# A transformer forward pass on one core: another order of smaller steps in the recurrence, matrix-memory and sliding-attention stages, and the causal mask added by TensorE

## The chip, the core and the metric

The kernel is one program on 1 core of a Trainium2 chip. Time is device time of that core in microseconds (us). The time before is 3654.07 us, the median of 3 runs (3653.0 to 3654.23). Each engine runs its own list of instructions: TensorE (PE in the profile) multiplies matrices into PSUM, VectorE (DVE) and ScalarE (ACT) do the rest of the arithmetic, and SyncE (SP) issues the DMAs. They wait for each other through semaphores only.

## The reference, cut to what matters

256 positions of width 1024, all in float32. Two layers of a first block, each a `token_mixing` and a feed-forward part, then four layers of a second block. All weights are used once.

```python
# first block, layers l = 0, 1: token_mixing (branches a, b, c, d), then a feed-forward part
proj = (rmsnorm(x, g_pre) * (1 + scale) + shift) @ w_in
p = causal_softmax(q1 k1^T / 8) - lam * causal_softmax(q2 k2^T / 8)   # a: 4 differential heads
ya = (rmsnorm(p v, g_subln) * (1 - lam_init)) @ da_w_o
q = [q_nope, rope(q_rope)]; k = [k_nope, rope(k_rope)]                # b: 8 latent heads, 64 + 32 wide
yb = (causal_softmax(q k^T / sqrt(96)) v_b) @ mla_w_o
yc = (sc_b * dwconv(sc_c * sc_u, 3 taps)) @ sc_w_o
yd = silu(layernorm(dwconv(cf_a * sigmoid(cf_g), 31 taps))) @ cf_w_o
x += gate1 * rmsnorm((g0*ya + g1*yb + g2*yc + g3*yd) @ w_mix_out)
# second block, layers n = 0..3
h = x + 0.5 * swiglu(rmsnorm(x));  h = h + mixer_n(rmsnorm(h));  h = h + 0.5 * swiglu(rmsnorm(h))
x = h + sigmoid(rmsnorm(h) @ w_ple_gate) * (p @ w_ple_proj)
# mixer 0 and 3, gated recurrence, 8 heads of 128, chunks of 64:
#   b = cumsum(log_f);  A[t,s] = sum_k q[t,k] k[s,k] exp(b[t,k] - b[s,k]) for s <= t
#   o = (q exp(b)) S + A v;  S = exp(b_last) S + (k exp(b_last - b))^T v
#   out = (rmsnorm(o) * silu(og)) @ w_out
# mixer 1, matrix memory, 4 heads: exponential input and forget gates, normalised by a running maximum
# mixer 2, sliding attention: 16 query heads, 4 key heads, window 128, distance bias, a sink per head
```

## The kernel before, in words

**Weights.** Every product is float32 by three passes. A weight tile of 128x1024 lands by a DMA of SyncE in one of 11 slots (`land`, NL, L278). ScalarE copies it into `whi`, one of 6 slots (NH; `split_scalar`, L401); VectorE subtracts that copy from the tile into `wlo` (`split_vector`, L413); TensorE multiplies high by high, high by low and low by high parts (`mm3`, L449 to L451). A "pair" is two such tiles: one projection of 128 rows of outputs over 256 positions, twice, 48 matmuls (`proj_tensor`, L466). To "take" a tile, ScalarE and VectorE split up to five tiles ahead (LOOK, L417; `take_scalar`, `take_vector`, L428), and the sixth slot is free only when TensorE has finished the tile that was in it.

**Steps.** The stages run one after the other: first block m0, f0, m1, f1 (mixing and feed-forward), then for n = 0 to 3 a half feed-forward (ha), the mixer (mx), the other half (hb) and the gate (pl). Within a mixer, all engines walk one list of steps: MIX (`mix_steps`, L891) for m0 and m1, HGRN (`hgrn_steps`, L1853) for mx0 and mx3, MLSTM (`mlstm_steps`, L2293) for mx1 and SWA (`swa_steps`, L2569) for mx2. Each engine issues its own instructions of a step in the order of the list and waits for events of others (`done` and `when`), so the list alone sets the order on TensorE, VectorE and ScalarE, and that of the weight tiles (`weight_order`, L3042). A PSUM bank's next writer waits for the event that its last user names (`Banks.use`, L177).

**Gated recurrence (HGRN).** Heads are worked in two groups of four. Per group: two pairs each for q (step q), the forget gate (f) and the values (v); `prepare` (wide elementwise work on decays); products across chunks, which use the state (`cross64`, `cross128`); seven `level` steps that build A by halves (ScalarE exponentials, VectorE differences and products, L2104 to L2119, small matmuls at L1942, and VectorE's mask and sum, L2254); `diagonal`; `values` (L1955). Then per head pair an output gate (gate, one pair), sums for the heads' norms (sum, L1965), `factor`, and `finish`, of which VectorE's low part is L1370. The norm ahead of the stage ends on TensorE at L1695. The order before, a dot standing for group and number:

```
norm q0.0 q0.1 f0.0 f0.1 v0.0 v0.1 prepare0 q1.0 cross64:0 q1.1 cross128:0 level0.0 f1.0 level0.1 f1.1 level0.2 v1.0
level0.3 v1.1 level0.4 0.5 0.6 diagonal0 values0 prepare1 sum0 sum1 factor0 cross64:1 gate0 cross128:1 level1.0 1.1 1.2
gate1 level1.3 finish0 level1.4 finish1 level1.5 gate2 level1.6 diagonal1 values1 sum2 sum3 factor1 gate3 finish2
finish3 end
```

**Matrix memory (MLSTM).** Projections qk (four pairs) and v (four), gate rows and columns, then per head `weights`, `scores`, `values`, `gate` and `tail` (norm and output gate of the head, L2528 to the low part at L1372), pipelined: gate i stands behind scores i+1, tail i behind values i. Order before: norm qk0 rows qk1 qk2 qk3 columns weights0 v0 v1 v2 v3 scores0 weights1 values0 scores1 weights2 values1 scores2 weights3 gate0 tail0 values2 scores3 gate1 tail1 values3 gate2 tail2 gate3 tail3 end.

**Sliding attention (SWA).** Three projections, per-head norm factors (`factor`) and transposes (`turn_in`, L2636) of them, then for each of 16 heads `scores` (L2646), `exp`, `turn` and `values`, and `heads` and `turn_out` at the middle and the end. Order before: norm proj0 columns proj1 factor0 turn_in0 factor1 turn_in1 proj2, then the heads, the four steps of a head one place apart.

**First-half mixers (MIX).** For each of four differential heads TensorE writes the scores of two blocks of 128 queries into 384 columns of a bank (L1065, L1066), VectorE adds a 384-column mask on the way out of PSUM (`softmax_vector`, L1357) and takes maxima from that copy (L1360, L1361), and ScalarE exponentiates it in place (`exp_scalar`, L1181). The bank is free after the mask addition ("masked"). Rope multiplies by a rotation in the bank MISC, which the norms' sums share (`rope_vector`, L1408, L1419); ScalarE's copies of the keys (L1321) follow the last rope.

Of the kernel before, what the change touches and what calls it, by code (L numbers as in the profile page):

```python
# [15 lines left out]
T = 256  # L16
# [28 lines left out]
def _plan_consts():  # L45
    at = 0
    for name, n in [("ident", 128), ("ones", 128), ("ones64", 128), ("mask3", 384), ("dist3", 384),
                    ("maskT", 128), ("lev", 192), ("rot", 96), ("inv", 1), ("rst", 256), ("spare", 15)]:
# [6 lines left out]
def constants():  # L55
# [10 lines left out]
    put("mask3", np.concatenate([causal, np.zeros((128, 128)), causal], 1))  # L66
# [195 lines left out]
class Program:  # L262


    def __init__(self, nc, ctx, args, order):
# [29 lines left out]
        self.sc = sb("sc", 16)  # L295
        self.ps = [ctx.enter_context(nc.psum_tensor(f"ps{i}", [128, 512], F32)) for i in range(8)]
# [262 lines left out]
def start_scalar(g, act):  # L559
# [3 lines left out]
    act.activation(g.small[:, 570:578], g.par[:, c:c + 8], ACT.Exp, scale=-1.0).then_inc(*D_("c_exp"))  # L563
    row_scalar(g, act)
# [326 lines left out]
def mix_steps():  # L891
# [27 lines left out]
    def merge(branch):  # L919
        return [[(f"wo{branch}", i), (f"gate{branch}", i)] for i in range(4)]  # L920
# [9 lines left out]
    for j in range(2):  # L930
        add("v", j)
        conv(2)
    add("tables")
    work = [[("mla", 0)], [("mla", 1)], [("mc", 0)]]
    work += alternate([[("mla_square", 0)], [("mla_norm", 0)], [("mla_square", 1)], [("mla_norm", 1)]],
                      [[("scu", j)] for j in range(4)] + [[("scb", j)] for j in range(2)])
    for n in range(2):
        work += [[("gate2", 2 * n)], [("gate2", 2 * n + 1)], [("wo2", 2 * n)], [("wo2", 2 * n + 1)]]
# [9 lines left out]
    add("ya_norm", 0)  # L948
    for r in range(4):
# [4 lines left out]
    add("ya_norm", 1)  # L954
    add("rope", 3)
# [8 lines left out]
    work = alternate([[("gate1", j)] for j in range(4)], [[("cf_mean", 0)], [("cf_norm", 0)]]) + merge(0) + merge(3)  # L964
    heads(8, ["mla_scores", "mla_scale", "mla_turn", "mla_values"], lambda: some(work, 1))
    some(work, len(work))
    for i in range(4):
        add("wo1", i)
    for j in range(4):
        add("out", j)  # L970
# [36 lines left out]
def mix_tensor(g, pe, st, lay):  # L1007
# [3 lines left out]
    for step, i, bank in MIX:  # L1011
# [42 lines left out]
        elif step in ("da_scores", "mla_scores"):  # L1054
# [4 lines left out]
            for m in range(2 if kind == "a" else 1):  # L1059
                b = 3 + m if kind == "a" else 3 + i % 2  # L1060
                pe.wait_ge(*W(*g.banks.use(b, "masked", st, kind, i, m)))
# [2072 lines left out]
```

## Time and profile before

| | |
|---|---|
| median of 3 runs | 3654.07 us |
| profiled execution, its own time | 3641.96 us |
| its span | 3639.9 us |
| mean granted TensorE clock | 0.948 |
| TensorE busy | 3291.6 us, 90% |
| VectorE busy | 2496.5 us, 69% |
| ScalarE busy | 1758.8 us, 48% |

| Stage | us in the span | TensorE idle, us |
|---|---|---|
| m0, m1 | 36.7 to 450.1, 659.1 to 1057.5 | 59.5, 52.1 |
| mx0, mx3 (gated recurrence) | 1446.0 to 1654.4, 3190.6 to 3405.2 | 50.7, 55.2 |
| mx1 (matrix memory) | 2071.9 to 2227.7 | 26.0 |
| mx2 (sliding attention) | 2645.9 to 2772.4 | 17.2 |

How to read it: the span is one profiled execution, from first to last instruction. Busy is the time in which an engine works on an instruction. The granted clock is a share of full speed, 2.4 GHz; 0.5 is 1.2 GHz. "x <- y" behind a time is what an engine waited for before it.

### The profile page before, as it was taken

Reading aid. Unit: us, or ns where it says so; the run is one execution under the profiler, and the core shown is the slowest. Engines: PE = TensorE matmul, PEld = TensorE weight load, DVE = VectorE, ACT = ScalarE, POOL = GpSimd, SP = SyncE. Lnnn points to the kernel's source line nnn. Section 1 sums busy time; section 2 is a strip of 40 time slices with the busy share of each in tenths; the row PEclk is TensorE's granted clock in tenths of the full one; section 3 lists DMA queues with packets and bytes.
Section 4 is the critical chain, followed back from the end, with each engine's and each line's share of the span. In section 5 each row is a group of like instructions: output and inputs, shape, how many; then the busy total and the mean of one; then the engine's idle time right before and its main releaser. Section 6 shows DMA issues by size and latency. Waiting matters only on the chain.

```text
span 3639.9 us, 64372 instructions
## 1 busy us (share of the span) xinstructions
PE 3291.6 (90%) x27058; PEld 3178.2 (87%) x27058; DVE 2496.5 (69%) x3768; ACT 1758.8 (48%) x2641; POOL 3.0 (0%) x6
## 2 busy tenths in 40 slices
PE   6788899887989999869999997999989999985898
PEld 6778899876989999759999987999968999985898
DVE  8877689886666766756676566666666666686656
ACT  4445444454544445555454445454455454464544
POOL 0000000000000000000000000000000000000000
PEclk9889999998999999979999999999989999997999
DMA  8444488443546565415656534655623655641453
GB/s 303 123 136 166 163 297 300 143 128 111 169 145 209 174 187 182 136 47 182 186 164 185 167 116 136 186 180 171 187 95 127 185 178 174 186 145 53 148 186 116
DMA packets 163920, 598.06 MB, mean 164 GB/s; under 512 B 18192, under 2 KB 18224, under 8 KB 163376
## 3 DMA queue, kind: packets, MB, share of 16 engines
q1 hardware_dynamic: 163632, 593.94, 51.1%
q8 instruction: 215, 3.52, 0.4%
q14 instruction: 73, 0.60, 0.1%
HBM read 592.82 MB, written 1.05 MB: 163 GB/s over the span
## 4 chain that ended last, share of the span: by engine, by line
PE 70%; DVE 21%; ACT 6%; issue 2%; DMA 1%; SPq 0%; DVEq 0%; ACTq 0%
PE ps L449 22%; PE ps L450 22%; PE ps L451 22%; DVE wlo L413 6%; DVE fa L1462 2%; ACT whi L401 2%; DVE hl L1666 1%; PE ps L622 1%; DVE land L506 1%; DVE tmps L530 0%; ACT L522 0%; DVE tmps L528 0%; DVE tmps L1804 0%; PE ps L712 0%; DMA land<-w_ada 0%
## 5 line engine op out<-in xcount | busy, mean ns | idle before, releaser
L449 PE MATMUL ps<-hh,whi 128*128 128x256 f32 (+1 forms) x5472 | 1561.4, 285 | 80.7 <-DVE hl L1666 32.8
L450 PE MATMUL ps<-hl,whi 128*128 128x256 f32 (+1 forms) x5472 | 1550.1, 283 | 0.0
L451 PE MATMUL ps<-hh,wlo 128*128 128x256 f32 (+1 forms) x5472 | 1545.1, 282 | 0.0
L413 DVE TENSOR_TENSOR wlo<-land,whi 128x1024 fp32r<-128x1024 f32 (+1 forms) x1032 | 1218.8, 1216 | 271.1 <-ACT whi L401 270.2
L449 PEld LDWEIGHTS ps<-hh,whi 128*128 128x128 f32 (+1 forms) x5472 | 1048.9, 192 | 93.3 <-issue 65.2
L401 ACT ACTIVATE whi<-land 128x1024 fp32r<-128x1024 f32 (+1 forms) x1032 | 1028.9, 1044 | 174.6 <-PE ps L451 161.5
L450 PEld LDWEIGHTS ps<-hl,whi 128*128 128x128 f32 (+1 forms) x5472 | 1048.9, 192 | 0.9
L451 PEld LDWEIGHTS ps<-hh,wlo 128*128 128x128 f32 (+1 forms) x5472 | 1048.0, 192 | 0.0
L449 PE MATMUL ps<-ra,whi 128*128 128x256 f32 (+1 forms) x2416 | 691.3, 286 | 29.6 <-DVE ra L1372 12.7
L451 PE MATMUL ps<-ra,wlo 128*128 128x256 f32 (+1 forms) x2416 | 688.4, 285 | 0.0
L450 PE MATMUL ps<-ra,whi 128*128 128x256 f32 (+1 forms) x2416 | 687.6, 285 | 0.0
L449 PEld LDWEIGHTS ps<-ra,whi 128*128 128x128 f32 (+1 forms) x2416 | 462.5, 191 | 32.6 <-DVE ra L1372 13.1
L450 PEld LDWEIGHTS ps<-ra,whi 128*128 128x128 f32 (+1 forms) x2416 | 460.5, 191 | 0.9
L451 PEld LDWEIGHTS ps<-ra,wlo 128*128 128x128 f32 (+1 forms) x2416 | 458.7, 190 | 0.0
L1730 ACT ACTIVATE tmps<-tmps 128x256 f32<-128x256 f32 x176 | 73.6, 418 | 592.4 <-DVE tmps L1754 592.4
L1754 DVE TENSOR_TENSOR tmps<-ps,small 128x512 f32<-128x512 f32 x176 | 121.4, 690 | 232.4 <-PE ps L451 232.2
L1370 DVE TENSOR_TENSOR ra<-tmps,ra 128x256 fp32r<-128x256 f32 x192 | 81.5, 424 | 89.2 <-ACT ra L1734 85.3
L1757 DVE TENSOR_TENSOR tmps<-tmps 128x256 f32<-128x256 f32 x176 | 74.9, 425 | 85.2 <-ACT tmps L1730 85.2
L506 DVE SCALAR_TENSOR_TENSOR land<-land,crow 128x1024 f32<-128x1024 f32 x96 | 116.3, 1218 | 6.1 <-ACT crow L572 5.8
L1734 ACT ACTIVATE ra<-tmps 128x256 fp32r<-128x256 f32 x176 | 73.7, 419 | 86.5 <-DVE tmps L1757 86.5
L1462 DVE SCALAR_TENSOR_TENSOR fa<-fa,par 128x256 f32<-128x256 f32 x240 | 97.5, 478 | 0.0
L829 ACT ACTIVATE fa<-tmps 128x256 f32<-128x256 f32 x44 | 18.4, 419 | 128.9 <-DVE tmps L858 128.9
(411 smaller groups left out, 2437.4 us busy)
## 6 DMA issues: line engine op xcount, KB each, us to landing
land<-w_gu SPq DMA_DIRECT2D x352, 512.0 KB, 3.6
land<-w_dn SPq DMA_DIRECT2D x176, 512.0 KB, 3.6
land<-w_in SPq DMA_DIRECT2D x136, 512.0 KB, 3.6
land<-w_ada SPq DMA_DIRECT2D x96, 512.0 KB, 3.7
land<-w_up SPq DMA_DIRECT2D x88, 512.0 KB, 4.2
land<-hg_in SPq DMA_DIRECT2D x64, 512.0 KB, 3.6
land<-w_down SPq DMA_DIRECT2D x44, 512.0 KB, 4.4
land<-ple_gate SPq DMA_DIRECT2D x32, 512.0 KB, 3.6
```

What stands on the lines that cost most here:

```text
L401: act.activation(w.hi, g.slot(n), ACT.Copy).then_inc(*D_("w_hi", n))
L413: dve.tensor_tensor(w.lo, g.slot(n), w.hi.bitcast(F32), ALU.subtract).then_inc(*D_("w_lo", n))
L449: pe.matmul(out, w.hi, x.hi, start=first, stop=False, skip_group_check=skip)
L450: pe.matmul(out, w.hi, x.lo, start=False, stop=False, skip_group_check=skip)
L451: return pe.matmul(out, w.lo, x.hi, start=False, stop=last, skip_group_check=skip)
L506: dve.scalar_tensor_tensor(w, w, 1.0, g.crow[:, :], ALU.mult, ALU.mult, accum_out=g.mod[:, i:i + 1]).then_inc(*D_("ada", i))
L1370: dve.tensor_tensor(out.lo, src, out.hi.bitcast(F32), ALU.subtract).then_inc(*D_(*event))
L1462: dve.scalar_tensor_tensor(o, M.cu[:, j, n:n + 256], g.P("cf_conv", lay * 124 + 4 * n + j), o, ALU.mult, ALU.add).then_inc(*D_("conv", st, ...
L1730: act.activation(b[:, 0:T], a[:, 0:T], ACT.Silu).then_inc(*D_("silu", st, j))
L1734: act.activation(R[p % 3].chunk(j % 2).hi, b[:, T:2 * T], ACT.Copy).then_inc(*D_("inner_hi", st, j))
L1754: dve.tensor_tensor(v2(a), v2(g.ps[4 + j % 3][:, :]), bc2(r), ALU.mult).then_inc(*D_("up_read", st, j))
L1757: dve.tensor_tensor(b[:, T:2 * T], b[:, 0:T], a[:, T:2 * T], ALU.mult).then_inc(*D_("prod", st, j))
```

## The change

Four things change, and the arithmetic is the same but for where the mask is added.

1. *Orders.* The rules that made the lists HGRN, MLSTM and SWA are replaced by lists written out. The steps are smaller: a step that took a pair and then wrote its result (q, f, v, gate, qk) becomes two, the taking (with TensorE's matmuls) and `_out` (with VectorE's and ScalarE's work on the result); the work for the token factors becomes steps `token` and `token_columns`. What VectorE has taken is kept in `held` for the later step. The first projecting step, whichever it is, waits for the norm's chunks (`ready`).
2. *MIX.* Its steps are cut in the same way (merge, mla_apply, ya_apply, cf_sum, cf_square, cf_apply, cf_silu, tables 0 and 1, sc_conv). The new parts stand next to each other, except that `sc_conv` comes ahead of the taking of its pair.
3. *Mask.* The constants hold one 128-column mask; ScalarE copies it and the identity to fp32r once at the start. Behind the scores of each diagonal block TensorE adds identity x mask into the same columns. VectorE's addition is gone, and maxima and exponentials read PSUM, so that the bank is freed by "exp". The wait for the buffer of probabilities moves from VectorE to ScalarE.
4. *Rope* uses banks 3 and 4 in turn in place of MISC.

The new orders and the core of the diff:

```diff
+HGRN_ORDER = """
+    norm:0.0 q:0.0 token:0.0 q:0.1 q_out:0.0 q_out:0.1 f:0.0 f_out:0.0 f:0.1 v:0.0 f_out:0.1 f:1.0 v:0.1 prepare:0.0
+    token_columns:0.0 v_out:0.0 q:1.0 cross64:0.0 q:1.1 level:0.0 level:0.1 level:0.2 q_out:1.0 level:0.3 q_out:1.1
+    level:0.4 f_out:1.0 v:1.0 f:1.1 level:0.5 f_out:1.1 level:0.6 v:1.1 cross128:0.0 diagonal:0.0 prepare:1.0
+    v_out:1.0 gate:0.0 gate:0.1 values:0.0 cross64:1.0 sum:0.0 sum:0.1 cross128:1.0 level:1.0 level:1.1 factor:0.0
+    level:1.2 gate_out:0.0 gate_out:0.1 level:1.3 finish:0.0 level:1.4 gate:0.2 level:1.5 level:1.6 gate:0.3
+    diagonal:1.0 gate_out:0.2 values:1.0 finish:0.1 sum:1.2 sum:1.3 factor:1.0 gate_out:0.3 finish:1.2 finish:1.3
+    end:0.0
+"""
+MLSTM_ORDER = """
+    norm:0 qk:0 token:0 qk_out:0 v:0 rows:0 qk:1 qk_out:1 qk:2 qk_out:2 qk:3 columns:0 qk_out:3 weights:0 v:1
+    v_out:0 scores:0 weights:1 v:2 weights:2 v:3 v_out:1 scores:1 values:0 values:1 weights:3 scores:2 gate:0
+    gate_out:0 tail:0 gate:1 gate:2 values:2 gate_out:1 tail:1 scores:3 gate:3 values:3 gate_out:2 gate_out:3 tail:2
+    tail:3 end:0
+"""
+SWA_ORDER = """
+    norm:0 proj:0 columns:0 factor:0 proj:1 factor:1 turn_in:0 proj:2 turn_in:1 exp:0 scores:0 scores:1 exp:1
+    scores:2 turn:0 factor:2 exp:2 scores:3 scores:4 values:0 turn:1 turn:2 values:1 turn_in:2 values:2 scores:5
+    exp:3 exp:4 scores:6 turn:3 exp:5 scores:7 turn:4 values:3 exp:6 scores:8 turn:5 values:4 exp:7 scores:9 turn:6
+    values:5 scores:10 exp:8 turn:7 values:6 exp:9 heads:0 turn:8 values:7 scores:11 exp:10 turn:9 values:8 turn:10
+    scores:12 turn_out:0 scores:13 exp:11 values:9 scores:14 exp:12 turn:11 values:10 exp:13 scores:15 turn:12
+    exp:14 values:11 turn:13 exp:15 values:12 turn:14 heads:1 values:13 turn:15 values:14 values:15 turn_out:1 end:0
+"""
...
         elif step == "gate":
-            n = take_vector(g, dve, "hg_in", *halves(j * 16 + 12 + i))
-            scaled_vector(g, dve, g.t(i % 2), ps, n, ("og_read", st, i))
+            held["gate", i] = take_vector(g, dve, "hg_in", *halves(j * 16 + 12 + i)), ps
+        elif step == "gate_out":
+            scaled_vector(g, dve, g.t(i % 2), *held["gate", i], ("og_read", st, i))
...
+        work += [... [("sc_conv", 2 * j), ("sc_conv", 2 * j + 1), ("scb", j)] for j in range(2)]
...
+    act.activation(g.causal[:, 0:128], g.C("ident", 0, 128), ACT.Copy)
+    act.activation(g.causal[:, 128:256], g.C("mask", 0, 128), ACT.Copy).then_inc(*D_("causal"))
...
-                pe.wait_ge(*W(*g.banks.use(b, "masked", st, kind, i, m)))
+                pe.wait_ge(*W(*g.banks.use(b, "exp", st, kind, i, m)))
...
+                for tb, end in ((0, 128), (1, 384)):
+                    pe.matmul(g.ps[b][:, tb * 128:end], q[p0:p1, a + tb * 128:a + tb * 128 + 128],
+                              k[p0:p1, a:a + tb * 128 + 128], start=True, stop=True)
+                    mm = pe.matmul(g.ps[b][:, end - 128:end], g.causal[:, 0:128], g.causal[:, 128:256], start=False,
+                                   stop=True, skip_group_check=True)
+                mm.then_inc(*D_("scores", st, kind, i, m))
...
-def exp_scalar(g, act, key, S, cols, scale):
+def exp_scalar(g, act, key, S, ps, cols, scale):
...
-    act.activation(S[:, 0:128], S[:, 0:128], ACT.Exp, bias=nm[:, 0:1], scale=scale, accum_out=sm[:, 0:1])
+    act.activation(S[:, 0:128], ps[:, 0:128], ACT.Exp, bias=nm[:, 0:1], scale=scale, accum_out=sm[:, 0:1])
...
-def softmax_vector(g, dve, key, S, ps, cols, scale):
+def softmax_vector(g, dve, key, ps, cols, scale):
...
-    dve.tensor_tensor(S, ps[:, 0:384], g.C("mask3", 0, 384), ALU.add).then_inc(*D_("masked", *key))
-    dve.wait_ge(*W("masked", *key))
-    dve.tensor_reduce(mx[:, 0:1], S[:, 0:128], AX, ALU.max)
-    dve.tensor_reduce(mx[:, 1:2], S[:, 128:384], AX, ALU.max).then_inc(*S_("vector_step"))
+    dve.tensor_reduce(mx[:, 0:1], ps[:, 0:128], AX, ALU.max)
+    dve.tensor_reduce(mx[:, 1:2], ps[:, 128:384], AX, ALU.max).then_inc(*S_("vector_step"))
...
-            pe.wait_ge(*W(*g.banks.use(MISC, "rot_sin", st, i)))
+            pe.wait_ge(*W(*g.banks.use(3 + i % 2, "rot_sin", st, i)))
```

## Rows read from the trace of the kernel before

**Rows 1.** The page: busy time of each engine, and the chain of waits by engine.
```profile
PE 3291.6 (90%) x27058; PEld 3178.2 (87%) x27058; DVE 2496.5 (69%) x3768; ACT 1758.8 (48%) x2641; POOL 3.0 (0%) x6
...
PE 70%; DVE 21%; ACT 6%; issue 2%; DMA 1%; SPq 0%; DVEq 0%; ACTq 0%
```

**Rows 2.** Windows: stretch, length, busy PE, PEld, DVE, ACT, POOL, clock, DMA share, GB/s.
```profile
36.70:450.10 413.40, 353.89 (x2568) 332.72 (x2568) 319.78 (x584) 196.80 (x328) 0.00 (x0) 0.90 0.49 162
1446.00:1654.40 208.40, 157.74 (x1793) 144.52 (x1792) 140.46 (x198) 112.90 (x169) 1.38 (x1) 0.85 0.32 99
1883.00:2071.90 188.90, 188.67 (x1569) 188.65 (x1570) 121.83 (x153) 90.39 (x126) 0.00 (x0) 0.98 0.58 179
2071.90:2227.70 155.80, 129.76 (x836) 111.22 (x836) 88.69 (x138) 70.01 (x95) 0.00 (x0) 0.95 0.34 105
2645.90:2772.40 126.50, 109.28 (x585) 90.38 (x584) 67.28 (x152) 62.31 (x154) 0.00 (x0) 0.82 0.24 80
```

**Rows 3.** Waits of TensorE, 1446.0 to 1654.4: us, times, the longest.
```profile
PE ps L1942 <- DVE attn L2119: 17.5, 4, 7.4
PE ps L1965 <- ACT fa L2068: 8.3, 2, 7.0
```

**Rows 4.** Groups of VectorE by line and shape, 1446.0 to 1654.4: busy, mean ns, idle before.
```profile
L413 DVE TENSOR_TENSOR wlo<-land,whi 128x1024 fp32r<-128x1024 f32 x36 | 42.4, 1220 | 18.7 <-ACT whi L401 18.5
...
L2110 DVE TENSOR_TENSOR fa<-fa 128x1024 f32<-128x1024 f32 x6 | 7.3, 1218 | 0.0
...
L2254 DVE TENSOR_TENSOR tmps<-ps,con 128x256 f32<-128x256 f32 x10 | 4.2, 418 | 0.5 <-PE ps L1942 0.5
...
L2117 DVE TENSOR_TENSOR fa<-fa 128x512 f32<-128x512 f32 x6 | 4.1, 684 | 0.7 <-ACT fa L1981 0.7
```

**Rows 5.** Timeline of TensorE in the first recurrence: start, duration, line, operation.
```profile
1453.62 0.60 PE L1695 MATMUL ps<-tmps,con 128*128 128x256 f32 x2
...
1553.87 0.64 PE L1955 MATMUL ps<-fa 128*128 128x128 f32 x2
```

**Rows 6.** Timeline of VectorE at the first recurrence's end; in brackets the wait before.
```profile
1632.58 0.69 DVE L1370 TENSOR_TENSOR ra<-fa,ra 128x512 fp32r<-128x512 f32 x1 [0.69 <-ACT ra L2081]
...
1637.48 0.69 DVE L1370 TENSOR_TENSOR ra<-fa,ra 128x512 fp32r<-128x512 f32 x1 [0.70 <-ACT ra L2081]
```

**Rows 7.** Window of levels and values in the first recurrence.
```profile
1528.00:1554.00 26.00, 16.82 (x295) 13.88 (x296) 17.13 (x25) 8.90 (x17) 0.00 (x0) 0.63 0.13 42
```

**Rows 8.** Matrix memory: timeline of its last tail, and TensorE's wait at the output.
```profile
2157.68 0.42 DVE L2528 TENSOR_SCALAR tmps<-ps 128x256 f32<-128x256 f32 x1
2158.32 1.28 ACT L520 ACT_TABLE_LOAD   x1
...
2165.48 0.69 DVE L1372 SCALAR_TENSOR_TENSOR ra<-fa,ra 128x512 fp32r<-128x512 f32 x1 [0.70 <-ACT ra L2443]
...
PE ps L449 <- DVE ra L1372: 12.7, 2, 10.0
```

**Rows 9.** Sliding attention: TensorE's waits, the first scores, a window of the loop's start.
```profile
PE ps L2636 <- DVE fa L2776: 6.0, 1, 6.0
PE ps L2636 <- DVE fa L2769: 3.5, 1, 3.5
...
2697.25 0.50 PE L2646 MATMUL ps<-fa 64*128 64x128 f32 x4
...
2699.00:2714.50 15.50, 12.79 (x48) 9.85 (x49) 9.38 (x30) 7.51 (x27) 0.00 (x0) 0.59 0.07 27
```

**Rows 10.** First-half mixer, 36.7 to 450.1: groups of VectorE, a wait, ScalarE's timeline.
```profile
L1357 DVE TENSOR_TENSOR attn<-ps,con 128x384 f32<-128x384 f32 x12 | 6.6, 552 | 2.6 <-PE ps L1066 2.4
...
L1360 DVE TENSOR_REDUCE small<-attn 128x1 f32<-128x256 f32 x12 | 4.9, 409 | 0.0
...
PE ps L1111 <- DVE tmps L1419: 5.8, 1, 5.8
...
264.37 0.59 ACT L1321 ACTIVATE fa<-ps 64x512 f32<-64x512 f32 x1 [4.44 <-DVE fa L1571]
```

More of the change, by code:

```diff
@@ L46, in _plan_consts @@
     at = 0
[L47 removed]
+    for name, n in [("ident", 128), ("ones", 128), ("ones64", 128), ("mask", 128), ("dist3", 384),
                     ("maskT", 128), ("lev", 192), ("rot", 96), ("inv", 1), ("rst", 256), ("spare", 15)]:
@@ L919, in merge @@
     def merge(branch):
-        return [[(f"wo{branch}", i), (f"gate{branch}", i)] for i in range(4)]
+        return [[(f"wo{branch}", i), (f"gate{branch}", i), (f"merge{branch}", i)] for i in range(4)]
     add("norm")
@@ L1805, in scaled_vector @@
     dve.wait_ge(*W(*event))
+HGRN_ORDER = """
[7 more added lines that the diff above has]
+"""
 def hgrn_steps():
[L1810 to L1812 removed]
+    steps, tiles = [], 0
+    for step in HGRN_ORDER.split():
+        name, at = step.split(":")
         bank = None
         if name in ("q", "f", "gate", "out"):
[L1815 to L1849 removed]
+            bank = tiles % 3
+            tiles += 1
+        steps.append((name, *[int(i) for i in at.split(".")], bank))
     return steps
@@ L2290, in head @@
         return [self.fa[:, a + s:a + e] for s, e in ((0, 384), (384, 768), (768, 1024), (1024, 1280))]
+MLSTM_ORDER = """
[4 more added lines that the diff above has]
+"""
 def mlstm_steps():
-    steps, count = [], [0]
-    def add(name, i=0):
+    steps, tiles = [], 0
+    for step in MLSTM_ORDER.split():
+        name, at = step.split(":")
         bank = None
         if name in ("qk", "gate"):
-            bank = count[0] % 3
-            count[0] += 1
-        steps.append((name, i, bank))
-    add("norm")
-    add("qk", 0)
-    add("rows")
-    for i in range(1, 4):
-        add("qk", i)
-    add("columns")
-    add("weights", 0)
-    for i in range(4):
-        add("v", i)
-    for i in range(7):
-        if i >= 3:
-            add("tail", i - 3)
-        if 1 <= i < 5:
-            add("values", i - 1)
-        if i < 4:
-            add("scores", i)
-            if i < 3:
-                add("weights", i + 1)
-        if 2 <= i < 6:
-            add("gate", i - 2)
-    add("end")
+            bank = tiles % 3
+            tiles += 1
+        steps.append((name, *[int(i) for i in at.split(".")], bank))
     return steps
@@ L2566 @@
 SWA_OUT = ((2, 6), (0, 1))
-def swa_steps():
-    steps = [("norm", 0), ("proj", 0), ("columns", 0), ("proj", 1), ("factor", 0), ("turn_in", 0), ("factor", 1),
-             ("turn_in", 1), ("proj", 2)]
-    work = [[("factor", 2)], [("turn_in", 2)]]
-    for i in range(19):
-        for s, name in ((3, "values"), (2, "turn"), (1, "exp"), (0, "scores")):
-            if 0 <= i - s < 16:
-                steps.append((name, i - s))
-        if i in (2, 4):
-            steps += work.pop(0)
-        if i == 10:
-            steps.append(("heads", 0))
-        if i == 12:
-            steps.append(("turn_out", 0))
-    steps += [("heads", 1), ("turn_out", 1), ("end", 0)]
-    return [s + (None,) for s in steps]
+SWA_ORDER = """
[6 more added lines that the diff above has]
+"""
+def swa_steps():
+    steps = []
+    for step in SWA_ORDER.split():
+        name, at = step.split(":")
+        steps.append((name, *[int(i) for i in at.split(".")], None))
+    return steps
 SWA = swa_steps()
```

353 lines of the change are left out of this document (181 added, 172 removed).

## The prediction

> **What bounds the kernel now.** I read the page's totals and its chain of waits first: TensorE is busy 90% of the span and carries 70% of the chain, VectorE 21%, DMA 1% [rows 1]. So time falls only where TensorE waits or runs at its lower clock. Then I read one stretch per stage [rows 2]. A feed-forward stage is the yardstick: 1569 matmuls in 188.7 us of 188.9, 0.12 us each, clock 0.98. Each first-half mixer (36.7 to 450.1, and 659.1 to 1057.5) leaves TensorE idle for 59.5 and 52.1 us; each gated recurrence (1446.0 to 1654.4, and 3190.6 to 3405.2) for 50.7 and 55.2 (of each pair the first is shown); the matrix memory for 26.0; the sliding attention for 17.2: 261 us of idle time in 1517. The clock there is 0.82 to 0.95. The reader is to see that VectorE, at 140 of 208 us in a recurrence, is not far behind: gaps can shrink, not vanish. The waits inside one recurrence name the links: 17.5 us for the products of a level in four waits, 8.3 for head sums in two [rows 3]; the rest are smaller ones of the same kinds and the diagonal's.
>
> **Gated recurrence, twice.** No arithmetic is added; the steps are cut in two (tiles taken, result written) and reordered. A pair of projection tiles is 48 matmuls, 48 x 0.12 = 5.8 us. A level costs VectorE one difference 1.22, two products 0.68 + 0.68, mask and sum 0.42 + 0.43: 3.4 us [rows 4]; it costs TensorE about 1.1 us at most. "Taking" a pair splits two tiles (2 x 1.22 on VectorE) and, by the six slots of whi and the look-ahead of five, waits until TensorE has finished the pair before.
>
> I laid the new order out by hand on these prices, from 1453.9, where TensorE has summed the norm [rows 5]. TensorE now has eight pairs (q1, f0, f1, v0, second f0, v1, second q0, q1) and the 64-column products before the first level: 46 + 1.5, so it reaches it at 1501.4. VectorE passes the take of v1 at 1486, then five wide operations of prepare (6.1), V (1.5), two takes (4.8) and 2.2: level 0 at 1500.7. They meet. Now five levels stand with no projection between: VectorE needs 3.4 each, and TensorE leaves the fifth at about 1513.5, of which some 9 us are idle. Then v0, f1, two levels, v1, the 128-column products and gates 0 and 1: 5 x 5.8 + 2.6 = 31.6, to 1545. That work covers the four things that stall today: the diagonal, prepare of the second group, and V. Values end at 1550; today they end at 1554.5 [rows 5], and two gates (11.6) are then done which today are not.
>
> Second group: first products, head sums and levels 0 to 4 to 1569 (again about 9 us idle, and 2 at the sums), gate 2, two levels, gate 3 to 1584, values to 1590, sums to 1594. VectorE then finishes heads 2 and 3 at 5 us each, as today (the low parts of the last two start at 1632.58 and 1637.48 [rows 6]): the last at 1605.6, against 1638.2 today. That is 32.6 us earlier.
>
> I don't believe all of it. TensorE is priced there at 0.12 us throughout, but today's stretch of levels and values from 1528 to 1554 has clock 0.63 (a mix of the levels 1.2 and 2.4 GHz) [rows 7], where only 16.8 of 26 us are busy. Five levels in a row are such a stretch, and two pairs of projections behind each run would take up to twice 11.6. Those behind the first run have slack of some 3 us; those behind the second do not. I take 10 us off: **22 us per recurrence, 44 for both**. Bounds: 10 (the clock stays low for all work after either run) and 33 (no tax).
>
> The page "TensorE: Matmul & The Clock Gate" of the Trainium skill (section "What's actually happening") says that the reduced clock is the resting state and that activity lifts it. This speaks against packing levels together; by it the order would lose part of what it gains, as in the third case below. The row at 0.63 agrees in kind.
>
> ScalarE's loads of function sets: 14 in this stretch today. In the new order two silu steps stand between exponentials of levels, but the silu steps come in pairs elsewhere; I count 12 to 13. Taken as nothing, -2.6 to +2.6 per recurrence (a load is 1.28 us [rows 8]); ScalarE, busy 112.9 of 208, hides it. The page "ScalarE: Activation LUTs" (section "What ACT_TABLE_LOAD costs") has about 2.66 us with its drain; the trace shows 1.28 [rows 8], with the next activation 0.02 behind. By the page the two extra switches in a level run would cost 5.3 us, mostly under VectorE's chain.
>
> The DMA order follows the new tile order. These stages move 99 and 105 GB/s [rows 2], a landing slot is asked for eleven tiles ahead, and no wait for a landing is among TensorE's: nothing.
>
> **Matrix memory.** The start gains: v:0 goes ahead of the gate rows, which removes the small waits at the norm, under 4 us. The end decides: a tail is one chain of 8.5 us on VectorE (from L2528 at 2157.68 to the low part ending 2166.17), its first part being two set loads with their activations [rows 8]. New: tail 1 ends about 2179.7, scores 3 next, values 3 end at 2182.3 with a wait of some 4.7; the two tails left follow each other, 2187.4 + 2 x 8.5 = 2204.4, against 2209.9 today. TensorE's idle 12.7 at the output [rows 8] becomes about 11. **5.5 us, with a little clock 6**; bounds 0 and 14 (if the tails' waits are filled).
>
> **Sliding attention.** factor:0 moves ahead of the second projection, turn_in behind it. Both waits, 6.0 and 3.5 us [rows 9], are then under 11.5 us of projection. Scores 0 starts at 2685 instead of 2697.25. Three scores before the first turn replace the 3.5 us wait by about 1. So 12 earlier, 3 more in the start of the loop. Three later waits, about 4 us together, stay. Clock: the loop's start runs at 0.59, 48 matmuls in 15.5 us [rows 9], and a later stretch is as slow; I keep both, less 1. **16 us**; bounds 9 and 28.
>
> **First-half mixers, twice.** The mask goes: 16 additions of 0.55 us on VectorE per layer, 8.9 us [rows 10]. The maximum now reads PSUM; no row has a reduction from PSUM, so between its 0.41 from SBUF and 0.55, what an addition over 384 columns with a PSUM source takes: 0 to 2 us per layer; I take 0. TensorE adds 32 matmuls of 128 columns; the nearest row is 0.12 for 256, so 0.06 to 0.12 each, 2 to 4 us per layer; I take 3, half of it in front of waits. A scores bank is freed only after the exponential: two activations, 0.40 + 0.49 plus the reads, about 0.9 later but without the 0.55. In the differential heads TensorE stands at that bank already, so +0.8 for two of four heads; in the latent heads the banks alternate: 0. Rope gets its own two banks, which ends the wait of 5.8 [rows 10] and two before it, 2.6 together. Late next: ScalarE copies mk only after kr_all, at 264.37 today and then too [rows 10], and TensorE needs that bank for its fourth ukv; so of 8.4 us only 2 are kept. VectorE's 8.9 us are spent mostly where it waits for ScalarE's split; they shorten the two waits at the layer norm (8.7 together) by about 2, and the taking by 1.5. Sum: 2 + 2 + 1.5 - 1.5 - 1 = **3 per layer, 6 for both**; bounds -5 and +8 each. The other cut steps there (mla, ya, cf, merge, tables) stand next to each other as before: nothing. Two casts of 128 columns at the start lie under ScalarE's wait for crow: nothing.
>
> **Sum.** 44 + 6 + 16 + 6 = 72 us off the profiled execution's 3641.96 (span 3639.9): 3570. The median shown is 12.1 above that execution; the same difference gives 3582.
>
> **Rivals.**
> (a) No clock tax and filled tails: 33 x 2 + 10 + 24 + 6 x 2 = 112, 3542. For it: most late waits of today are single links. Against: 0.63 at 1528.
> (b) The level runs park TensorE and keep it at 1.2 GHz into the gates: 10 x 2 + 3 + 12 + 0 = 35, 3619. For it: the clock of [rows 7]. Against: gates 0 and 1 follow behind 17 us of dense pairs.
> (c) VectorE, not TensorE, is the bound in mixers: gaps move without shrinking, 3654 within 7. For it: 140 and 320 busy. Against: in those stages it idles too, 68 and 94 us.
> (d) Slower: the bank held until the exponential. If each of 32 softmaxes made TensorE wait the full 0.9 and the mask matmuls added 4 per layer, that is 37 us on the attention parts; it decides where the reordering brings less, as it would in (c): 3685. Against: banks alternate and pairs of 5.8 us stand between.
>
> **How the numbers follow.** Forecast 0.50, (a) 0.17, (b) 0.20, (c) 0.06, (d) 0.07. About 0.2% (7 us) is what a measurement of this kernel can tell from no change. Faster 0.88 (the first three and a little of (c)), same 0.04, slower 0.08. The forecast's own range, from the middle of the bounds, is 3560 to 3605; with (a) and (b) taken in, 3535 to 3628.
>
> **What would show it.** Right: sliding attention's scores starting some 12 us earlier after its first projection; each recurrence 15 to 30 us shorter, with two idle runs of about 9 us among levels and none at the diagonal; TensorE's wait at the matrix memory's output still near 10. Wrong: clock under 0.8 over a whole recurrence (b), new waits on ScalarE's exponentials at the scores (d), or a last finish not before 1625 in the first recurrence, which would say that VectorE was the limit.

## The result, and the profile after

| | before | after |
|---|---|---|
| median of four timed runs each | 3654.15 us | 3534.02 us (3525.52 to 3548.07) |
| ratio | | 0.9674, 95% interval 0.9638 to 0.971 |
| profiled execution, its own time | 3641.96 us | 3540.5 us |
| its span, clock | 3639.9, 0.948 | 3538.7, 0.954 |

The change takes 120 us off the median and 101.5 off the profiled execution; 72 were forecast. The time lies just under the stated range (3535 to 3628), and beside the first rival's 3542. The two differences lie 18.7 apart: the old kernel's profiled execution is 12.2 under its median, and the changed kernel's is 6.5 over its own. In the latter sliding attention was slow; a second profiled execution of the same kernel (run *again*) took 3530.35. By stage, in us:

| Stage | before | after | again | forecast saving |
|---|---|---|---|---|
| m0, m1 | 413.4, 398.4 | 405.2, 391.6 | 409.0, 392.6 | 3 each |
| mx0, mx3 | 208.4, 214.6 | 174.2, 178.5 | 174.8, 179.4 | 22 each |
| mx1 | 155.8 | 148.5 | 148.7 | 6 |
| mx2 | 126.5 | 120.2 | 102.8 | 16 |

The page of the changed kernel, busy time and chain [rows 1]:

```profile
PE 3280.9 (93%) x27122; PEld 3174.9 (90%) x27122; DVE 2479.0 (70%) x3736; ACT 1752.6 (50%) x2641; POOL 3.0 (0%) x6
...
PE 74%; DVE 18%; ACT 5%; issue 2%; DMA 1%; SPq 0%; DVEq 0%; ACTq 0%
```

Its windows of the stages of [rows 2], in that order, and last the middle of the head loop:

```profile
36.10:441.30 405.20, 355.28 (x2600) 333.32 (x2600) 311.19 (x568) 195.37 (x328) 0.00 (x0) 0.93 0.48 165
1430.00:1604.20 174.20, 146.25 (x1793) 136.95 (x1793) 140.37 (x198) 111.63 (x169) 1.39 (x1) 0.90 0.34 119
1832.90:2021.30 188.40, 187.22 (x1569) 187.20 (x1570) 122.84 (x155) 91.30 (x128) 0.00 (x0) 0.98 0.52 179
2021.30:2169.80 148.50, 130.68 (x836) 112.25 (x836) 88.78 (x138) 69.60 (x94) 0.00 (x0) 0.94 0.32 110
2588.40:2708.60 120.20, 115.54 (x586) 98.03 (x586) 67.34 (x153) 62.03 (x155) 0.00 (x0) 0.76 0.24 84
...
2634.00:2684.00 50.00, 49.33 (x199) 40.63 (x198) 23.00 (x64) 24.13 (x87) 0.00 (x0) 0.50 0.00 1
```

Two things are to be seen. In the recurrence VectorE does the same 140 us of work, but TensorE's busy time fell from 157.7 to 146.3 with the same matmuls: 22.7 of the 34.2 us are waits that went, 11.5 are what the same matmuls were busy less at a higher clock (0.90 for 0.85). In sliding attention it is the other way: 12.6 us of waits went, and 6.3 came back as busy time, because the clock was lower (0.82 to 0.76): it was 0.50 for the whole of a 50 us stretch in which TensorE was busy 49.3.

TensorE's waits in the first recurrence, after [rows 3] (us, times, the longest):

```profile
PE ps L1959 <- DVE fa L2139: 11.7, 4, 3.6
PE ps L450 <- DVE ra L1394: 6.2, 2, 3.1
PE ps L1959 <- DVE attn L2139: 4.8, 3, 2.3
PE ps L1982 <- ACT fa L2088: 3.5, 2, 2.3
PE ps L1982 <- DVE fa L2120: 1.8, 2, 0.9
```

The diagonal and `cross64` (7.1 and 2.9 before) are gone from the list, and no wait is longer than 3.6. VectorE's last low part there, which answers to [rows 6]:

```profile
1585.81 0.69 DVE L1394 TENSOR_TENSOR ra<-fa,ra 128x512 fp32r<-128x512 f32 x1 [0.70 <-ACT ra L2101]
```

It ends 156.5 us after the stage's start; before, the last one ended 192.2 us after it.

### The profile page after: what moved, and what is told of

The parts are those of the page before. It is cut to its first block, busy times and chain, and to the rows that moved or that the text cites. A ratio compares the mean times of both kernels' runs of the same rounds, so it can differ in the third digit from the quotient of the medians.

```text
span 3538.7 us, 64480 instructions
## 1 busy us (share of the span) xinstructions
PE 3280.9 (93%) x27122; PEld 3174.9 (90%) x27122; DVE 2479.0 (70%) x3736; ACT 1752.6 (50%) x2641; POOL 3.0 (0%) x6
## 4 chain that ended last, share of the span: by engine, by line
PE 74%; DVE 18%; ACT 5%; issue 2%; DMA 1%; SPq 0%; DVEq 0%; ACTq 0%
PE ps L450 23%; PE ps L451 23%; PE ps L452 23%; DVE wlo L414 5%; DVE fa L1486 2%; ACT whi L402 1%; DVE hl L1701 1%; PE ps L626 1%; DVE land L507 1%; ACT L523 1%; PE ps L1194 1%; DVE tmps L531 0%; DVE tmps L529 0%; PE ps L716 0%; DMA land<-w_ada 0%
```

## The experiments

Each is the changed kernel with one edit; "again" is it itself. The first four ran on one chip, the next four below them in the table on another, then rope_old, kr_early and hgrn_tail, then best, each group beside its own runs of the kernel before (medians 3650.9, 3644.8, 3654.3 and 3655.8), so small effects are read from the stages and not from the totals.

| Run | median us (range) | ratio to before |
|---|---|---|
| again | 3529.99 (3525.84 to 3530.36) | 0.9677 |
| hgrn_old | 3594.86 (3593.43 to 3612.74) | 0.9874 |
| swa_old | 3554.06 (3543.82 to 3560.94) | 0.9743 |
| swa_fill | 3528.26 (3527.07 to 3531.85) | 0.9676 |
| hgrn_spread | 3554.96 (3552.5 to 3561.01) | 0.9758 |
| hgrn_fill | 3534.82 (3532.02 to 3551.96) | 0.9709 |
| mask_old | 3535.15 (3534.5 to 3535.4) | 0.9699 |
| mlstm_old | 3533.94 (3532.22 to 3534.12) | 0.9695 |
| rope_old | 3531.12 (3525.06 to 3547.2) | 0.9679 |
| kr_early | 3522.99 (3518.62 to 3523.74) | 0.9644 |
| hgrn_tail | 3534.32 (3532.87 to 3549.44) | 0.9687 |
| best | 3500.54 (3499.23 to 3500.94) | 0.9587 [0.9563, 0.9611] |

**again.** No edit.

> The changed kernel once more, unchanged, beside the others on one chip. Theory A: the spread of its four runs so far (3525.5 to 3548.1) comes from TensorE's clock, so its times again differ by 10 to 20 us, and in the profile the sliding attention (120 us in the first profile, 55 us of it at the clock 0.50 with TensorE busy throughout) is the stage that differs most. Theory B: the spread is that of the chip; then every stage differs by the same share, and the other kernels of this call scatter as much.

Theory A for the stages, not for the times: its four runs differ by 4.5 us where 10 to 20 were expected. The stages agree within 4 us but one: sliding attention took 102.8 us where the first profile had 120.2. Windows of this run, the head loop and the stage:

```profile
2640.60:2690.60 50.00, 46.89 (x316) 41.19 (x316) 31.33 (x76) 30.92 (x96) 0.00 (x0) 0.88 0.11 34
2594.90:2697.70 102.80, 97.15 (x585) 83.00 (x585) 67.05 (x152) 61.16 (x154) 0.00 (x0) 0.93 0.30 98
```

In 50 us 316 matmul records in place of 199, from the same instructions in the same order. Eleven profiled executions here (the changed kernel's two and nine of the kernels below) have this stage unchanged: it took 102.4 to 103.2 us in nine of them and 120.1 to 120.2 in two, the first and hgrn_tail's. In the traces the clock is 0.50 for 58.0 us on end in these two, and for 10.2 us in each of the nine.

**hgrn_old.** The old order, in the new small steps.

```diff
-HGRN_ORDER = """ norm:0.0 q:0.0 token:0.0 q:0.1 q_out:0.0 q_out:0.1 f:0.0 ...
+HGRN_ORDER = """ norm:0.0 q:0.0 token:0.0 q_out:0.0 q:0.1 q_out:0.1 f:0.0 f_out:0.0 ...
```

> The changed kernel with the old order of the gated recurrence, in the new small steps; all else as changed. Theory A (the order alone is what the recurrences gain by, and it also lifts the clock there): mx0 and mx3 go back to 207 to 215 us from 174 and 178, the granted clock in them from 0.90 to 0.85, and the whole takes 65 to 75 us longer than the changed kernel. Theory B (part of the gain there comes from what stands around the recurrences, such as where the tiles taken ahead stand): the stages come back to 195 to 205 only, 40 to 50 us.

Theory A, in full: mx0 and mx3 take 208.2 and 215.0, the median rises by 64.9 (at the lower end of what was expected), and the window is that of [rows 2] again, to 0.3 us in each engine:

```profile
1430.00:1638.20 208.20, 157.86 (x1793) 144.63 (x1792) 140.56 (x198) 112.93 (x169) 1.39 (x1) 0.85 0.31 100
```

**hgrn_fill.**

```diff
@@ hgrn_tensor, step "level", ahead of the waits for the level's products; the bank's wait moves there too
+            pe.wait_ge(*W(*g.banks.use(3 + i % 2, *(("level_out", st, gr, i) if i else ("level0_out", st, gr)))))
+            for _ in range(16 if i < 5 else 0):
+                pe.matmul(ps[:, 0:T], g.causal[:, 0:128], g.causal[:, 0:T], start=True, stop=True)
...
-            pe.wait_ge(*W(*g.banks.use(3 + i % 2, *(("level_out", st, gr, i) if i else ("level0_out", st, gr)))))
```

> The changed kernel with 16 more matmuls of 128x256 ahead of each of levels 0 to 4 in both groups, issued while TensorE waits for VectorE there, into the bank that the level then overwrites; same output. Theory A (the low clock in the runs of levels costs nothing, because VectorE sets the pace there and the clock is back before the projections end): the clock in the runs is 1.00, the stage stays at 174 within 1 us or grows by up to 3. Theory B (the projections behind the runs pay a tax of up to 5 us each, as the prediction held): the stage falls by 4 to 10 us per recurrence.

In time this is theory A. First the changed kernel's two runs of levels, then this kernel's two and its stage:

```profile
1485.00:1500.00 15.00, 6.98 (x282) 5.92 (x276) 13.38 (x21) 10.12 (x17) 0.00 (x0) 0.70 0.11 37
1541.00:1556.00 15.00, 7.84 (x214) 7.54 (x215) 13.95 (x21) 12.20 (x22) 0.00 (x0) 0.54 0.01 2
```

```profile
1490.50:1505.50 15.00, 14.53 (x373) 13.51 (x372) 11.53 (x18) 7.59 (x14) 0.00 (x0) 1.00 0.14 50
1547.00:1562.00 15.00, 14.41 (x354) 13.53 (x348) 13.53 (x20) 12.26 (x21) 0.00 (x0) 1.00 0.01 3
1436.00:1611.90 175.90, 161.37 (x1954) 151.71 (x1953) 140.48 (x198) 111.74 (x168) 1.39 (x1) 0.98 0.38 118
```

The clock is 1.00 through both runs, and the stages are 1 to 3 us longer than without (175.9 and 181.1).

But this doesn't show that the low clock costs nothing, because the fill has a price of its own. Windows of the first pair behind each run of levels show both parts, the changed kernel's two and then this kernel's:

```profile
1496.71:1504.44 7.73, 7.73 (x31) 6.15 (x25) 6.34 (x14) 7.60 (x10) 0.00 (x0) 0.71 0.18 66
1551.34:1559.08 7.74, 7.74 (x55) 7.70 (x48) 6.77 (x13) 6.23 (x8) 0.00 (x0) 0.71 0.20 67
```

```profile
1505.07:1510.74 5.67, 5.67 (x25) 4.59 (x25) 4.83 (x10) 5.57 (x8) 0.00 (x0) 1.00 0.30 73
1558.97:1564.69 5.72, 5.72 (x56) 5.67 (x48) 4.78 (x9) 4.24 (x7) 0.00 (x0) 1.00 0.25 75
```

Within a run the low clock costs little: VectorE, busy 13.4 and 13.9 of 15 us, sets the pace there. The pair behind it takes 2.0 us longer at the low clock. The fill takes these 2.0 us away, but with it TensorE leaves the fifth level 2.1 us later in the first group and 1.5 in the second, counted from the sum of the norm. After the first run the two kernels are level again (level 5 starts 72.4 and 72.5 us after that sum); after the second the pair ends early and TensorE waits 1.6 us for VectorE.

So a gain of 2.0 us and a cost of 2.1 us stand against each other in the first group. That the 2 us behind the first run are on the path is seen in the run again: there that pair took 7.1 us in place of 7.7, and level 5, the values and the last low part all came some 0.6 us earlier. The low clock of the two runs costs about 2 us per recurrence, at most 4, where the prediction took 10. The Trainium skill ("TensorE: Matmul & The Clock Gate", section "What's actually happening") says that activity releases the throttle; the rows agree (0.70 and 0.54 without the fill, 1.00 with it).

**hgrn_spread.** The same tiles in the same sequence, with projections between levels.

```diff
-    level:0.0 level:0.1 level:0.2 q_out:1.0 level:0.3 q_out:1.1 level:0.4 f_out:1.0 v:1.0 f:1.1 level:0.5 f_out:1.1 level:0.6 v:1.1
+    level:0.0 v:1.0 level:0.1 q_out:1.0 level:0.2 q_out:1.1 level:0.3 f_out:1.0 f:1.1 level:0.4 level:0.5 f_out:1.1 v:1.1 level:0.6
...
-    gate_out:0.0 gate_out:0.1 level:1.3 finish:0.0 level:1.4 gate:0.2 level:1.5 level:1.6 gate:0.3
+    gate_out:0.0 gate:0.2 level:1.2 gate_out:0.1 level:1.3 finish:0.0 gate:0.3 level:1.4 level:1.5 level:1.6
```

> The changed kernel, but in each recurrence the projections that stand behind a run of levels are put between them (v1.0 behind level 0, f1.1 behind level 3, gates 2 and 3 behind levels 1 and 3 of the second group); the same work. Theory A (gathering the levels in runs of five is itself worth something, since TensorE then idles at the low clock in one place and all projections run at the full one): TensorE's idle time in the runs shrinks from 16 us to some 8, but the clock dips in more places, VectorE's takes (2.4 us each) land in its chain of levels, and the stage is 3 to 10 us longer than 174. Theory B (the gain comes only from having projections under VectorE's long steps, wherever the levels stand): the stage is as long or shorter, 166 to 174 us.

Outside both theories: the stage takes 187.1 (and 195.6 in mx3), 13 and 17 us more, and TensorE's idle time grew instead of shrinking, from 28 to 39.6.

```profile
PE ps L1959 <- DVE attn L2139: 18.4, 5, 8.2
PE ps L450 <- DVE tmps L1839: 6.2, 1, 6.2
```

L1839 writes the result that frees f:1.1's bank. Put between levels, this projection waits for an output step that stands behind four levels on VectorE; in the changed kernel a whole pair stands between that output step and the projection. The order's worth is in what VectorE has finished when TensorE asks for it. The clock is not the reason (0.88, against 0.90). The run changes the place of four pairs at once, so the share of each stays open.

**hgrn_tail.**

```diff
-    level:1.6 gate:0.3 diagonal:1.0 gate_out:0.2 values:1.0 finish:0.1 sum:1.2 sum:1.3 factor:1.0 gate_out:0.3 finish:1.2
+    level:1.6 diagonal:1.0 gate_out:0.2 values:1.0 finish:0.1 sum:1.2 sum:1.3 gate:0.3 factor:1.0 finish:1.2 gate_out:0.3
```

> The changed kernel, but in each recurrence the last gate's pair stands behind the last head sums in place of ahead of the diagonal, and head 2 is finished ahead of that gate's output. Theory A (VectorE's chain to the last low part sets the end of the stage, and the pair can as well cover the two head finishes): diagonal and values start about 2.4 us earlier, TensorE's waits of 6.2 us at the output nearly go, and each recurrence is 3 to 5 us shorter. Theory B (the take of the gate only moves to a later place of the same VectorE chain): less than 1 us.

A miss: about 2 us longer per recurrence (176.4 and 181.3). The waits show a new one of 5.3 at the diagonal, which the pair had covered:

```profile
PE ps L1970 <- ACT fa L2078: 5.3, 1, 5.3
PE ps L450 <- DVE ra L1394: 4.4, 1, 4.4
```

**swa_old.** The old order of sliding attention.

```diff
-SWA_ORDER = """ norm:0 proj:0 columns:0 factor:0 proj:1 factor:1 turn_in:0 proj:2 turn_in:1 exp:0 scores:0 ...
+SWA_ORDER = """ norm:0 proj:0 columns:0 proj:1 factor:0 turn_in:0 factor:1 turn_in:1 proj:2 scores:0 ...
```

> The changed kernel with the old order of sliding attention. Theory A (the new order takes 12.5 us of waits away and gives 6 of them back, because the head loop now runs its first 55 us at the clock 0.50): the stage takes about 126 us, TensorE idle 17 and the clock 0.82, so 6 us longer than the changed kernel's 120. Theory B (clock in the loop is luck of the run and not of the order): the stage takes between 115 and 140 and its clock does not follow the order.

The waits of [rows 9] come back, and the stage takes 122.9 with TensorE idle 17.3:

```profile
PE ps L2654 <- DVE fa L2794: 6.1, 1, 6.1
PE ps L2654 <- DVE fa L2787: 3.6, 1, 3.6
PE ps L1194 <- ACT attn L2731: 3.5, 1, 3.5
```

Against the run again the stage is 20.1 longer, 11.6 of it idle time and 8.5 busy time (clock 0.86 against 0.93), and the median 24.1. So the order is worth 20 to 24 us against the usual case of the new one, though this is one execution of the old order, whose four runs spread by 17 us. The 6.3 of the first profile is the slow case of a stage whose clock is not the order's alone: theory A holds for the waits, theory B for the clock.

**swa_fill.**

```diff
@@ swa_tensor, step "scores", behind the wait for the bank
+            for _ in range(32 if i == 5 else 0):
+                pe.matmul(ps[:, 0:T], g.causal[:, 0:128], g.causal[:, 0:T], start=True, stop=True)
```

> The changed kernel with 32 more matmuls of 128x256 ahead of the scores of head 5 in sliding attention, into the bank that these scores then overwrite; the output is the same. Theory A (the clock is low there because the heads' small matmuls do not ask for it to rise, and dense work lifts it): the 32 cost 4 to 7 us, the clock is 1.00 behind them, 11 heads take 2.1 us instead of 3.7, and the stage falls from 120 to 105 us or less. Theory B (the loop is bound by ScalarE and VectorE, or the clock falls back at once): the stage grows by the 4 to 7 us.

```profile
2588.60:2695.00 106.40, 100.75 (x618) 86.55 (x617) 67.29 (x153) 61.20 (x153) 0.00 (x0) 0.94 0.29 95
2640.00:2690.00 50.00, 47.57 (x343) 42.36 (x342) 26.79 (x62) 29.44 (x91) 0.00 (x0) 0.95 0.14 42
```

106.4 us: 14 less than the slow case, 3.6 more than the usual one. Since nine of eleven executions without fill have the clock back by themselves, this one can't decide between the theories. That the fill would help where the clock stays low is not shown: none of its four runs is over 3531.9, but four are few.

**mlstm_old.** The old order of the matrix memory.

```diff
-MLSTM_ORDER = """ norm:0 qk:0 token:0 qk_out:0 v:0 rows:0 qk:1 qk_out:1 ...
+MLSTM_ORDER = """ norm:0 qk:0 token:0 qk_out:0 rows:0 qk:1 qk_out:1 ...
```

> The changed kernel with the old order of the matrix memory. Theory A (the order brings what the two profiles differ by): mx1 takes 155 to 156 us instead of 148.5, and TensorE idles 26 us there instead of 18; the whole is 7 us longer. Theory B (part of it is clock luck): mx1 between 148 and 153.

157.7 us against 148.5, idle 25.8 against 17.8: theory A, somewhat more than said. The changed kernel's waits there, and then this kernel's:

```profile
PE ps L450 <- DVE ra L1396: 7.9, 2, 5.4
PE ps L2392 <- DVE fa L2526: 6.7, 1, 6.7
PE ps L2410 <- DVE tmps L2546: 2.2, 1, 2.2
```

```profile
PE ps L450 <- DVE ra L1396: 12.5, 2, 10.1
PE ps L2410 <- DVE tmps L2546: 4.7, 1, 4.7
PE ps L2392 <- DVE fa L2526: 4.5, 3, 2.9
```

**mask_old.**

```diff
-                    mm = pe.matmul(g.ps[b][:, end - 128:end], g.causal[:, 0:128], g.causal[:, 128:256], start=False, ...
-                pe.wait_ge(*W(*g.banks.use(b, "exp", st, kind, i, m)))
+                pe.wait_ge(*W(*g.banks.use(b, "masked", st, kind, i, m)))
+    dve.tensor_tensor(S, ps[:, 0:384], g.C("mask3", 0, 384), ALU.add).then_inc(*D_("masked", *key))
```

> The changed kernel with the mask added by VectorE again: 384 columns out of PSUM, maxima and exponentials from that copy, the bank free after the addition, and no mask matmuls. Theory A (the mask's move is what the first-half mixers gain by): m0 and m1 are 5 to 8 us longer each. Theory B (VectorE's 8.9 us were mostly time in which it would have waited anyway, and the 32 mask matmuls, at 0.38 us each in the profile, 12.2 us per layer, take as much from TensorE): m0 and m1 change by less than 2 us each, and the whole by less than 4.

m1 takes 397.0 against 391.6 and 392.6, m0 410.4 against 405.2 and 409.0. That is theory A, at its lower end, in m1; in m0 the changed kernel's own two executions differ by 3.8, so that m0 says little. Windows of both, the kernel with the mask on VectorE and then the changed one, m1:

```profile
656.00:1053.00 397.00, 343.85 (x2568) 325.61 (x2568) 291.39 (x528) 193.57 (x324) 0.00 (x0) 0.94 0.45 141
```

```profile
650.00:1041.60 391.60, 350.13 (x2600) 330.62 (x2600) 282.81 (x511) 191.97 (x324) 0.00 (x0) 0.94 0.42 143
```

With the 32 mask matmuls TensorE is busy 6.3 us longer, and 11.7 of its idle time go with VectorE's 8.6. (The busy time of this stage differs by some 4 us between executions of the same instructions, so read 6.3 as 4 to 8.) Which waits they were is in the two lists for m1, first with the mask on VectorE, then after:

```profile
PE ps L449 <- DVE wlo L413: 6.3, 4, 3.4
...
PE ps L1088 <- ACT tmps L1206: 5.3, 1, 5.3
```

```profile
PE ps L450 <- DVE wlo L414: 2.8, 3, 1.5
...
PE ps L1094 <- ACT tmps L1212: 1.2, 1, 1.2
```

L1088 and L1094 are the same product, the values of a differential head. The wait of the latent heads at their values is as good as unchanged (1.5 and 1.3).

**rope_old.**

```diff
-            pe.wait_ge(*W(*g.banks.use(3 + i % 2, "rot_sin", st, i)))
+            pe.wait_ge(*W(*g.banks.use(MISC, "rot_sin", st, i)))
```

> The changed kernel with rope's products in the one shared bank again. Theory A (the own banks removed real waits, and half of them came back at the wait for ScalarE's copies of the keys): m0 and m1 are 1 to 3 us longer each than the changed kernel's 405 to 409 and 392. Theory B (all of it came back later): m0 and m1 the same within 1 us; the waits before the rotations return (3 to 8 us) and the wait of 9.3 us at the fourth product of the keys is that much shorter.

Theory B: 409.1 and 392.1 against 409.0 and 392.6 of the run again (the first profile has 405.2 for m0, so m1 is the stage to go by). The wait before the rotation is back (5.8 in m0, 6.7 in m1, the line below), and in this kernel's list no wait for the copies of the keys is left, where the changed kernel has 9.3 and 9.1. One takes the place of the other.

```profile
PE ps L1126 <- DVE tmps L1443: 6.7, 1, 6.7
```

**kr_early.**

```diff
     add("ya_norm", 1)
-    add("ya_apply", 1)
     add("rope", 3)
+    add("ya_apply", 1)
     add("rope", 4)
```

> The changed kernel, but in the first-half mixers the fourth rope stands between the norm factor of the differential heads' second half (ya_norm 1) and its use (ya_apply 1), where VectorE waits 2.6 us for ScalarE. Theory A (TensorE's wait of 9.3 us for ScalarE's copies of the keys is the end of VectorE's chain up to kr_all, so what is filled there is saved): the wait falls to 6.5 to 7.5 us and m0 and m1 are 2 to 3 us shorter each. Theory B (TensorE's wait is held up by ScalarE's own order, or the gain is lost at the first latent scores): less than 1 us.

The wait fell from 9.3 to 7.3 (m0) and from 9.1 to 7.1 (m1); m1 takes 388.8, 3 to 4 less. The median is 3523.0, and its range lies under that of the run again.

**best.** kr_early, and the layer norm's steps taken apart:

```diff
-    work = alternate([[("gate1", j)] for j in range(4)], [[("cf_sum", 0), ("cf_mean", 0)],
-                                                              [("cf_square", 0), ("cf_norm", 0), ("cf_apply", 0), ("cf_apply", 1),
-                                                               ("cf_silu", 0), ("cf_silu", 1)]]) + merge(0) + merge(3)
+    work = [[(f"cf_{s}", 0), ("gate1", j)] for j, s in enumerate(("sum", "mean", "square", "norm"))]
+    work += [[("cf_apply", 0), ("cf_apply", 1), ("cf_silu", 0), ("cf_silu", 1)]]
+    work += merge(0) + merge(3)
```

> The kernel with the fourth rope moved (as in the run before), and with the layer norm's four small steps (cf_sum, cf_mean, cf_square, cf_norm) each put ahead of one of the four gate pairs in place of two by two. TensorE's two waits there, 2.7 and 4.8 us per layer, each come from a VectorE sum over 1024 columns (1.9 us) that stands directly ahead of TensorE's product. Theory A (a projection pair between the sum and the product covers them): both waits fall under 1 us, m0 and m1 are 5 to 7 us shorter each than with the rope alone (403.6 and 388.8), the whole is 10 to 14 us shorter, near 3512. Theory B (the latent heads' chain through VectorE and ScalarE sets the pace of that stretch, and the waits only move to the heads' transposes): less than 3 us per layer.

```profile
36.20:429.10 392.90, 349.74 (x2600) 328.92 (x2600) 311.01 (x568) 194.91 (x328) 0.00 (x0) 0.95 0.49 171
637.10:1015.30 378.20, 346.65 (x2600) 327.87 (x2600) 282.72 (x512) 191.59 (x324) 0.00 (x0) 0.95 0.43 148
```

Both waits (L1156 and L1161 in the changed kernel, 2.7 and 4.8 per layer) are gone from the lists. m0 and m1 take 10.7 and 10.6 less than with kr_early, where 5 to 7 were expected. In m1 8.2 of it is idle time and 2.4 busy time; in m0 only 4.6 is idle time and 6.0 busy time, at a clock of 0.95 in place of 0.92. With 3500.5 us this is the fastest of all, 0.9587 of the kernel before.

## Why the prediction was right and where it was wrong

- **That the recurrences bring most of it: right.** hgrn_old gives 64.9 of the 120 us back.
- **The layout by hand: right.** Counted from the stage's start, TensorE was to reach level 0 at 55.4 and leave the fifth level at 67.5; it did at 54.6 and 66.8. Values were to end at 104 and ended at 102.0, the last low part at 159.6 and stood at 155.8 to 156.5. The idle time in each run of five levels was put at 9 us and was 8.0 and 8.5. ScalarE's loads of function sets: 13, of the 12 to 13 counted.
- **"I take 10 us off": wrong.** This is the step that failed. The tax is real but small: the first pair behind each run of levels took 7.7 us where 5.7 is its time at the full clock (hgrn_fill), so 2.0 twice, of which the second may be hidden. "Up to twice 11.6" had the clock low for two whole pairs, and the 10 taken was of that size. The slack was also the other way round: behind the first run TensorE does not wait again before the head sums, and behind the second it waits for VectorE once the clock is full (hgrn_fill). The old order paid such a tax too, and a larger one: its waits were strewn over the stage and the work next to them ran slow, the same matmuls being busy 11.5 us longer than now, and the clock over the whole recurrence rose from 0.85 to 0.90. Gathered into two runs, most waits slow down only the levels' own small products, where VectorE sets the pace. The layout, which priced the new order at 0.12 us per matmul and took the old one's times as they were, had this gain in it already. With 2 to 4 us off in place of 10 it would have said 29 to 31; the two recurrences gained 34 and 36. Of the 12 and 14 us by which they beat the forecast, 6 to 8 are this step; 3 more show in the last low part of the first recurrence, which came that much ahead of the layout.
- **Sliding attention: the waits right, the clock wrong.** Scores 0 started 39.0 us after the stage's start against 51.3, the 12 earlier that were forecast. "I keep both, less 1", said of the two slow stretches, had a wrong premise: that the clock belongs to the place. It was 0.50 for 50 us of the head loop in one execution and 0.88 over the same stretch in another. The stage's saving is 24 in the usual case and 6 in the slow one; the 16 forecast lie between, which no execution showed.
- **Matrix memory: right**, 7.3 for 6, with 7.9 waiting at the output where about 11 were said and 6.7 at the values where 4.7 were.
- **First-half mixers: direction right, size too small.** 3 per layer were forecast; the two profiles show 4 to 8 for m0 and 6 to 7 for m1. Of the terms, "2 kept of 8.4" for rope was too much: rope_old shows nothing kept that can be told from none. The mask was put at 2 + 1.5 for VectorE's share, less 1.5 for the matmuls and 1 for the bank, so +1; mask_old shows 4.4 to 5.4 in m1. Its matmuls cost about twice the 3 us taken, and 11.7 us of TensorE's idle time went, more than VectorE's whole 8.9. The maximum from PSUM costs nothing, as taken: 0.414 us, beside 0.409 in [rows 10]:

```profile
L1384 DVE TENSOR_REDUCE small<-ps 128x1 f32<-128x256 f32 x16 | 6.6, 414 | 0.0
```

- **Rivals.** (a), no clock tax, came nearest: its 112 us are 33 per recurrence, 10, 24 and 6 per mixer, and the second profile shows 34 and 35, 7, 24, and 4 and 6. (b) fell with the clock, which was back within the first pair behind each run of levels, and (c) with TensorE's idle time, 50.7 to 28.0 us in the first recurrence. (d): the bank held until the exponential does show, as one wait of 6.5 in m0 (L1078, for ScalarE's L1203), where 5.2 stood for the mask's addition; 1.3 more in one place, not 0.9 in each of 32. (Its 37 us on top of 3654 would have been 3691, and not the 3685 that it gave.) The wait:

```profile
PE ps L1078 <- ACT attn L1203: 6.5, 1, 6.5
```

- **"The same difference gives 3582": wrong.** The old kernel's profiled execution lies 12.2 below its median, the changed kernel's 6.5 above, and the second one 0.4 above. The old kernel's runs beside the experiments spread from 3636.9 to 3661.4, with mean clocks of 0.941 to 0.951, so one execution tells the median to some 12 us only. With (a)'s 112 us the profile gives 3530, which is what the second execution took; with the 12 on top it gave 3542.

## What to carry to other kernels

Where one engine feeds another through a chain of small steps, put the chain in one run and the dense work behind it, so that each wait falls where the other engine sets the pace anyway; count what the first projection behind the chain pays in clock (2.0 us here); then look at what stands directly between a sum and its reader, as the layer norm here, and put one projection there. Price the clock of the old order as well as that of the new before taking a tax off. Read a stage from more than one profiled execution before ascribing a few us to an edit.

## What the runs showed of the hardware that was not expected

TensorE's clock can stay at the lower of its two levels while its record shows it busy almost throughout. In the first profile it was granted 0.50 over 50 us of the head loop with TensorE busy 49.3, for 199 matmul records; in the second, of the same instructions, it came back after 10.2 us (0.88 over the same stretch, 316 records), and nine of eleven executions took that course. The page "TensorE: Matmul & The Clock Gate" of the Trainium skill, section "What's actually happening", says that the throttle depends on how busy the engine has been. Here busy time in the record did not tell the two cases apart: it was 49.3 of 50 us where the clock stayed low and 46.9 where it came back, in part because a matmul's record is longer at the low clock (behind the levels above, 0.63 us against 0.40 for 512 columns). What sets the course is not shown; with dense matmuls in the middle of the loop (swa_fill) the clock was 0.95, which the usual case comes near without them.

A mask matmul of 128 columns lasts 0.37 us in its record in m1, but with 32 of them the busy time of m1 is only 6.3 us longer, 0.2 each, and still more than the 0.06 to 0.12 taken from larger ones. With the spread of that stage's busy time it is 0.13 to 0.25 each.
